# Down projections with the activations held still: 512 weight columns moving, sums kept with tokens on partitions and turned at the end of each MLP

## The reference, cut to what matters

```python
def squared_relu_mlp(hn, w_up, w_down):
    return jnp.square(jax.nn.relu(hn @ w_up)) @ w_down
...
        h = h + mix
        h = h + squared_relu_mlp(rms_norm(h, norm_mlp_g[i]), w_up[i], w_down[i])
        gate = jax.nn.sigmoid(rms_norm(h, norm_ple_g[i]) @ w_ple_gate[i])
        h = h + (p[i] @ w_ple_proj[i]) * gate
```

## Time and profile before

| what | value |
|---|---|
| runs, median of 3 | 2349.45 us (2348.93 to 2349.71) |
| profiled execution, first to last instruction (span) | 2346.1 us |
| profiled execution's own time | not listed apart from its span; the runs' median is 3.35 us above the span |
| TensorE busy | 2324.9 us, 99% |
| VectorE, ScalarE busy | 1534.6 us (65%), 1252.6 us (53%) |
| mean granted TensorE clock | 0.998 |

### The profile page before, as it was taken

One profiled execution on the slowest core, in us unless ns is written; L12 is line 12 of the kernel. 1 busy time (PEld: TensorE's weight loads), 2 busy tenths in 40 slices (PEclk: granted clock), 3 DMA queues, 4 the chain that ended last, 5 costly groups with the idle time before them and its releaser, 6 DMA issues.

```text
span 2346.1 us, 39851 instructions
## 1 busy us (share of the span) xinstructions
PE 2324.9 (99%) x13964; PEld 2078.5 (89%) x13964; DVE 1534.6 (65%) x1848; ACT 1252.6 (53%) x1616; POOL 77.1 (3%) x73
## 2 busy tenths in 40 slices
PE   8999999999999999999999999999999999999998
PEld 7999998888888888888888888888888888888887
DVE  8899776556556555668676666765555555556666
ACT  6876655445445435556666666555444444445454
POOL 0046100000000000000000000000000000000000
PEclk9999999999999999999999999999999999999999
DMA  8555465655655665665555555565556556556553
GB/s 254 181 181 161 154 206 172 195 179 190 194 189 182 191 199 179 188 205 174 186 179 157 176 170 177 180 190 179 189 196 188 180 194 198 179 184 202 186 166 122
DMA packets 432334, 431.24 MB, mean 184 GB/s; under 512 B 13312, under 2 KB 430208, under 8 KB 432256
## 3 DMA queue, kind: packets, MB, share of 16 engines
q1 hardware_dynamic: 431968, 429.97, 58.1%
q10 hardware_dynamic: 288, 0.23, 0.0%
HBM read 428.05 MB, written 2.10 MB: 183 GB/s over the span
## 4 chain that ended last, share of the span: by engine, by line
PE 97%; DVE 1%; ACT 1%; DMA 1%; issue 0%; DVEq 0%; ACTq 0%; SPq 0%
PE ps L492 54%; PE ps L498 28%; PE ps L533 3%; PE ps L534 3%; PE ps L535 3%; PE ps L490 2%; PE ps L497 1%; PE O L803 1%; DVE spl L1337 1%; DMA raw<-in_w_o 0%; PE O L654 0%; PE Z L628 0%; ACT spl L861 0%; PE Z L637 0%; PE ps L707 0%
## 5 line engine op out<-in xcount | busy, mean ns | idle before, releaser
L1337 DVE TENSOR_TENSOR spl<-raw,spl 128x1024 fp32r<-128x1024 f32 x797 | 938.6, 1222 | 579.5 <-ACT spl L861 572.2
L861 ACT ACTIVATE spl<-raw 128x1024 fp32r<-128x1024 f32 (+1 forms) x811 | 817.3, 1054 | 686.5 <-PE ps L498 593.7
L492 PE MATMUL ps<-XA,spl 128*128 128x512 f32 x2816 | 705.0, 392 | 7.3 <-DVE spl L1545 6.7
L492 PE MATMUL ps<-XB,spl 128*128 128x512 f32 x2784 | 711.5, 392 | 0.0
L492 PEld LDWEIGHTS ps<-XA,spl 128*128 128x128 f32 x2816 | 505.1, 189 | 91.5 <-issue 7.4
L492 PEld LDWEIGHTS ps<-XB,spl 128*128 128x128 f32 x2784 | 491.4, 188 | 75.6
L498 PEld LDWEIGHTS ps<-XB,spl 128*128 128x128 f32 x2784 | 394.5, 191 | 39.0
L498 PEld LDWEIGHTS ps<-XA,spl 128*128 128x128 f32 x2816 | 387.3, 191 | 31.4
L498 PE MATMUL ps<-XB,spl 128*128 128x256 f32 x2784 | 402.6, 281 | 0.0
L498 PE MATMUL ps<-XA,spl 128*128 128x256 f32 x2816 | 393.8, 282 | 0.0
L1373 DVE TENSOR_TENSOR tv<-cross,ps 128x512 f32<-128x512 f32 x181 | 123.2, 681 | 13.2 <-ACT cross L861 13.0
(11 more groups left out here) (207 smaller groups left out, 1531.6 us busy)
## 6 DMA issues: line engine op xcount, KB each, us to landing
raw<-in_w_up SPq DMA_DIRECT2D x256, 512.0 KB, 4.8
raw<-in_w_down SPq DMA_DIRECT2D x256, 512.0 KB, 5.2
raw<-in_w_qkv SPq DMA_DIRECT2D x96, 512.0 KB, 4.4
raw<-in_w_gate SPq DMA_DIRECT2D x64, 512.0 KB, 4.6
raw<-in_w_in SPq DMA_DIRECT2D x63, 512.0 KB, 4.7
raw<-in_w_out SPq DMA_DIRECT2D x32, 512.0 KB, 3.6
raw<-in_w_o SPq DMA_DIRECT2D x32, 512.0 KB, 4.8
raw<-in_w_proj SPq DMA_DIRECT2D x8, 512.0 KB, 4.1
```

What stands on the lines that cost most here:

```text
L492: pe.matmul(ps[:, b + o, :], w[:, q, 0, c], x[:, kt, :, :], start=start, stop=False)
L861: return act.activation(out, in_, ACT.Copy, scale=scale)
L1337: dve.tensor_tensor(s[:, :, 1, :], raw[:, m % NRAW, :, :], s[:, :, 0, :].bitcast(F32), ALU.subtract).then_inc(lo_ready, 1)
```

## The change

The 256 down-projection chunks become 2 x 128 rows of 512 output columns. The hidden activations are now stationary (128 tokens at a time), and 512 weight columns move: 12 matmuls a chunk, each with 512 moving columns. The result has tokens on the partitions, 512 channels wide. For each 512 channels and each quarter, DVE alone takes it out of PSUM into a buffer `acc` in SBUF (`collect`: a copy in the first quarter, an addition after that). In the last quarter TensorE turns `acc` in 128 x 128 blocks (`turn`: eight transposes for 512 channels, 32 a layer), DVE adds the turned block from PSUM to `h` (`take_turned`), and the residual chain follows. The turn of one block of 512 channels stands in the middle of the next block's matmuls; the last one stands between steps j = 1 and j = 2 of the gate's `first_pair`.

```diff
 def down(f):                                     # SP
     with sp.Fori(0, 4) as i:
-        for s in range(2):
-            load_group(m + 32 + 4 * s, f * 8 + i, w_down[layer], i * 512 + 256 * s, row0=f * D)
+        for c in range(8):
+            src = w_down[layer, bass.ds(f * D + 2 * c * P, 2 * P), bass.ds(i * 512, 512)]
+            load(m + 32 + c, f * 8 + i, src.rearrange("(t p) n -> p t n", p=P))
...
+def down(s, m, it, hid, tiles, mid=None):        # PE
+    b = 2 * s
+    for c in range(8):
+        if c == 4 and mid is not None:
+            mid()
+        if tiles is not None:
+            pe.wait_ge(*tiles[c])
+        lo_there(pe, m + c, it)
+        w = spl[:, (m + c) % NSPL, :, :, :]
+        for q in range(2):
+            for t in range(2):
+                x = [hid[:, 2 * c + q, k, t * P:(t + 1) * P] for k in range(2)]
+                for n, (xh, wh) in enumerate(((0, 0), (1, 0), (0, 1))):
+                    mm = pe.matmul(ps[:, b + t, :], x[xh], w[:, 2 * q:2 * q + 2, wh, :],
+                                   start=(c == 0 and q == 0 and n == 0), stop=(c == 7 and q == 1 and n == 2))
+        mm.then_inc(chunk_used, 1)
+
+def turn(g, hidx, i):                            # PE
+    pe.wait_ge(sum_ready, g + 56 + 2 * i + 2)
+    for k in range(2):
+        if hidx + 2 * i + k >= 2:
+            pe.wait_ge(res_ready, hidx + 2 * i + k - 1)
+        for j in range(2):
+            for t in range(2):
+                c = (4 * i + 2 * k + j) * P
+                mm = pe.transpose(O[:, k, j * T + t * P:j * T + (t + 1) * P], acc[:, t, c:c + P], ident[:, :])
+        mm.then_inc(turned, 1)
...
+    for i in range(4):                           # PE, last quarter
+        pe.wait_ge(sum_ready, g + 54 + 2 * i)
+        tiles = [(up_tiles, u + 24 + c + 1) for c in range(8)] if i == 0 else None
+        down(i % 2, m + 224 + 8 * i, 0, hid, tiles, None if i == 0 else lambda: turn(g, hidx, i - 1))
...
-    first_pair(g, m, x, after_res(f_in), lambda: stats(norm))
+    first_pair(g, m, x, after_res(f_in), lambda: stats(norm), mid=lambda: turn(*last, 3), sums=g - 2)
...
+    for i in range(4):                           # ACT, last quarter
+        for q in range(8):
+            split(m + 224 + 8 * i + q + NSPL)
+            if i > 0 and 4 <= q < 6:
+                k = 2 * i + q - 6
+                residual((res_ready, hidx + k + 1), hidx + k, 2 * k, n, X)
...
+def collect(s, m, it, col, before, fresh):       # DVE
+    dve.wait_ge(chunk_used, it * 8 + (m + 8))
+    if not fresh:
+        dve.wait_ge(sum_ready, before)
+    for t in range(2):
+        a = acc[:, t, bass.ds(col, 512)]
+        if fresh:
+            r = dve.tensor_copy(a, ps[:, 2 * s + t, :])
+        else:
+            r = dve.tensor_tensor(a, a, ps[:, 2 * s + t, :], ALU.add)
+        r.then_inc(sum_ready, 1)
...
+def take_turned(hidx, k, f, n, X):               # DVE
+    dve.wait_ge(turned, hidx // 24 * 8 + k + 1)
+    ht = h[:, 2 * k:2 * k + 2, :]
+    dve.tensor_tensor(ht, ht, O[:, k % 2, :].rearrange("p (o n) -> p o n", o=2), ALU.add).then_inc(res_ready, 1)
+    dve.wait_ge(res_ready, hidx + k + 1)
+    residual(f + k, 2 * k, n, X)
...
+    for i in range(4):                           # DVE, last quarter
+        for q in range(8):
+            if q == 7:
+                collect(i % 2, m + 224 + 8 * i, 0, 512 * i, g + 40 + 2 * i + 2, False)
+            split(m + 224 + 8 * i + q + NSPL)
+            if i > 0 and 4 <= q < 6:
+                take_turned(hidx, 2 * i + q - 6, f_out, n, X)
...
-gates(G_GATE0, C_GATE0, 0, 24, H_GATE0, 2, 3, XB)                # DVE; ACT alike
+gates(G_GATE0, C_GATE0, 0, 24, H_GATE0, 2, 3, XB, {
+    4: lambda: take_turned(H_MLP0, 6, 16, 2, XA), 5: lambda: take_turned(H_MLP0, 7, 16, 2, XA)})
```

More of the change, by code:

```diff
@@ L67 @@
 CHUNKS = 812
[L69 removed]
+H_MLP0, H_GATE0, H_OUT1, H_MLP1, H_GATE1 = 0, 8, 16, 24, 32
 NDG = 22
@@ L290, in crossed @@
         def crossed(g):
-            return g - (32 if g >= G_MLP0 else 0) - (8 if g >= G_OUT1 else 0)
+            return g - sum(n for first, n in ((G_MLP0, 32), (G_GATE0, 32), (G_OUT1, 8), (G_GATE1, 32)) if g >= first)
         def lo_there(engine, m, it):
@@ new lines, in mlp, with ups, downs @@
+            def mlp(g, m, x, hid, f_in, norm, u, hidx):
+                def ups(f):
+                    whole(g, f * 16, m, f * 8, x, sums=f * 16 + (g - 2))
+                    whole(g + 1, f * 16, m + 4, f * 8, x)
+                    with pe.Fori(1, 4) as i:
+                        for s in range(2):
+                            whole(g + s, f * 16 + i * 2, m + 4 * s, f * 8 + i, x)
+                def downs(f):
+                    with pe.Fori(0, 2) as j:
+                        for s in range(2):
+                            pe.wait_ge(sum_ready, f * 16 + j * (3 + s) + (g + 7 + s))
+                            tiles = [(up_tiles, f * 8 + (u + c + 1)) for c in range(8)] if s == 0 else None
+                            down(s, m + 32 + 8 * s, f * 8 + j * 2, hid, tiles)
@@ L943, in up, with gate @@
                 copy(hid[:, bass.ds(t0, 2), 0, :], tv[:, :, :]).then_inc(up_hi, 1)
-            def gate(g, gi, m, it, k, hidx, t0, n, X, norm_n=None, first=False):
-                group(g, gi, m, it, first, 2)
+            def gate(g, gi, m, it, k, hidx, t0, n, X, norm_n=None, first=False, steps={}):
+                group(g, gi, m, it, first, 2, steps)
                 if norm_n is not None:
@@ L975, in mlp @@
                 with act.Fori(0, 4) as i:
-                    for s in range(2):
-                        group(g + 8 + s, i * 2, m + 32 + 4 * s, i)
+                    period(m + 32, i, 8)
                 with act.Fori(1, 3) as f:
@@ L1349, in period, with group @@
                     split(m + NSPL + q, it)
-            def group(g, gi, m, it, first=False, later=0, steps={}):
+            def group(g, gi, m, it, first=False, later=0, steps={}, ci=None):
                 if not first:
@@ L1432, in up, with proj @@
                 dve.wait_ge(up_tiles, u + 1)
-            def down(g, gi, m, it, hidx, t0, first=False, later=0, steps={}):
+            def proj(g, gi, m, it, hidx, t0, first=False, later=0, steps={}):
                 group(g, gi, m, it, first, later, steps)
@@ L1459, in out_groups @@
                     for s in range(2):
-                        down(g + s, 0, m + 4 * s, 0, hidx + s, 2 * s, True, steps=first)
+                        proj(g + s, 0, m + 4 * s, 0, hidx + s, 2 * s, True, steps=first)
                         residual(f + s, 2 * s, n, X)
@@ L1469, in mlp @@
                 for s in range(2):
[L1470 removed]
+                    up(g + s, 0, 0, m + 4 * s, 0, u + s, 2 * s, hid, norm_in if s == 0 else None, True)
                 with dve.Fori(1, 4) as i:
                     for s in range(2):
[L1473 to L1476 removed]
+                        up(g + s, i * 2, i * 2, m + 4 * s, i, i * 2 + (u + s), i * 4 + 2 * s, hid)
+                downs(g, m, 0, True)
                 with dve.Fori(1, 3) as f:
```

123 lines of the change are left out of this document (55 added, 68 removed).

## The result

The changed kernel takes **2355.57 us** (median of 9 runs, 2353.74 to 2357.02), the kernel before 2349.45 us in the runs beside it (9 runs): a ratio of 1.0025, 95% interval 1.0016 to 1.0035. The forecast was 2357.6 us with a range of 2350 to 2368, so the sign and the size came out. How they came about did not follow the forecast in every step, and errors of opposite sign partly cancelled each other.

What follows compares the result with a forecast made beforehand. The prediction took TensorE's matmul stream as the bound. Matmuls -12.4, transposes +5.3 and waits at the gate +15.2 gave +8.1 us, a span of 2354.2 us and, with 3.35 us above the span, 2357.6 us (range 2350 to 2368).

Steps and rivals of the forecast that it cites:

- Part 1: Down matmuls on TensorE: 12 of 227.5 ns a chunk replace 16, saving 48.5 ns in each of 256 chunks, -12.4 us.
- the prediction's own sign of being wrong: Down matmul spacing other than 227.5 ns, no wait at the gate, or waits in the quarters before would show it wrong.
- Part 2: Transposes on TensorE: one pass each at 0.11 us, 48 in the open over two layers, +5.3 us.
- Part 3: Sums on ACT and DVE: both lose work, hidden in idle time; no collection waited for in the first three quarters.
- Part 4: Last down quarter and gate's start: queued DVE and ACT work makes TensorE wait 7.6 us per layer, +15.2 us.
- Wait A: Gate's second chunk waits 2.4 us a layer for the PSUM pair that DVE is still collecting.
- wait B: Gate's step j = 3 gets its input 5.2 us later; TensorE spends 0.9 on turn(3) and waits 4.3.
- the step on the clock: At the gate, TensorE's granted clock was to be still 1.00 behind the second wait, of about 4.3 us.
- this fall as a rival: TensorE's clock falls at the gate in both layers, costing up to 2 x 2.5 us: 2362.6 us; chance 0.10.
- Two passes: Each transpose on TensorE takes two passes, 0.22 us, 10.6 us in all: 2362.8 us; chance 0.20.
- Waits covered: Gate waits cost nothing and all 64 transposes count: -5.4 us, 2344.1 us; chance 0.17, in whole or part.
- A gap in the moving operand: Down matmuls moving two runs of 256 columns pay for the gap: up to +37 us, 2394 us; chance 0.03.

Runs made afterwards that it cites:

- The first two experiments: Changed kernel with turn(0) to turn(2) ahead of the third down chunk, not the fifth: 2352.29 us; changed kernel with only turn(3) one gate step earlier: 2344.18 us.
- the first experiment: Changed kernel with turn(0) to turn(2) ahead of the third down chunk instead of the fifth, residual chains moved likewise, turn(3) unmoved: 2352.29 us, ratio 1.0011.

## Why the prediction was right, point by point

- **Part 1 was mis-sized, the mechanism held.** Four matmuls less a chunk is a gain that nothing covers, and weights move no slower than activations. No gap cost showed up in the moving operand. The gain is 15.0 us instead of 12.4. For the chunk after I took 227.5 ns for each matmul from blocks of 32, whose start behind 256 columns is slow, and a stream of 384 runs at 226.75. A difference of 0.3% in a term that stands 3072 times in the kernel is 2.3 us, nearly what the whole change weighs in a layer (2.86). By the letter, the prediction's own sign of being wrong, a spacing other than 227.5, came true. The terms as written also give 47.6 ns a chunk, not 48.5; that takes the 2778.6 ns of 689.10 us for 248 chunks, and the down chunks alone took 2779.4.
- **Part 2 held.** One pass, and the price was right: 0.11 us, taken from line 628 rather than from line 727, although 727 has the type and the shape; 0.113 with the matmul behind, 0.109 for one more. 48 open transposes are 5.4 us, forecast 5.3. The page of the Trainium skill weighed there ("TensorE: Matmul & The Clock Gate", section Terms) has a transpose mode four times as fast for FP32, and does not say than what. The trace does not bear out the estimate made of it, a quarter of 0.22 us or 0.055: a transpose costs half of the 0.22.
- **Part 3 held.** DVE and ACT lose work, there is no wait in the first three quarters, and loads in wider rows (packets down from 432,334 to 366,810 on the two pages) bring TensorE no wait for a chunk in the stretch.
- **Part 4 held in mechanism, and both waits were forecast too long.** Wait A costs 1.48 us a layer instead of 2.4 (1.33 of wait and 0.15 of starting again), wait B 4.5 instead of 5.2 (with the eight transposes that it covers), because the queue of DVE repeats every 4.30 us and not 4.73. The first two experiments show each wait alone, by taking it away.
- **What failed is the step on the clock**, "granted clock still 1.00 behind the second". I had this fall as a rival at 0.10 and up to 2.5 us a layer. It came, in both layers, at 1.67 us (2.5 in one layer of the first experiment, so the price I gave was the upper end). The row for it was on the table: 0.70 some 4 us after dense work ended, and a wait B of 4.3 us. No row spoke against it. It should have been in the sum.
- **The other rivals.** Two passes: refuted. Waits covered: not in this kernel, but reached by moving the turns. A gap in the moving operand: refuted by 226.75 ns, where moving activations without a gap settle at 226.8.

Put together by what was measured: -15.0 + 48 x 0.113 + 2 x (1.48 + 4.5 + 1.67) = +5.7 us, which is what the two stretches show. The forecast was +8.1: matmuls and the two waits were too dear by 2.6, 1.8 and 1.4, the transposes too cheap by 0.1, and the clock was missing with 3.3. So the total was nearer than its terms: the missing clock hid more than half of what the others had too much, and that is luck.

## What to carry to other kernels

A cheaper matmul stream can lose all its gain at the one place where its results have to get back into the layout of the next stage: here -15.0 us became +6.1, and moving the same instructions two chunks and one step ahead made it -7.5. So when results leave TensorE by a longer way, count the queue of the engines that carry them (period by period, from start to start), and place the work so that the last consumer still has that long. Where an idle wait of TensorE like wait B (3.5 us here) can't be avoided, add the lower clock behind it to its price (1.7 to 2.5 us here), or try needless matmuls that fill it. And take a price from a whole stretch with and without the thing: the window of 0.79 us around eight transposes missed an eighth of their cost.

## What the runs showed of the hardware

- A plain float32 transpose of 128 x 128 is one instruction, while a plain float32 product of the same shape is two. In a stream it costs 0.109 us, 0.113 with the matmul behind that is followed late. Its own record says 273 ns. The Trainium skill ("TensorE: Matmul & The Clock Gate", Part 4 on the transpose) gives about 275 ns for one in bf16 in a kernel; the trace agrees for float32.
- In the changed kernel the clock falls not in the wait but after it: TensorE works for 1 us at 1.00 and then at a mean of 0.53 for 3.6 us. What that costs is not fixed. With wait A gone (the first experiment) the clock fell within the same wait B in the first layer, a mean of 0.79 in the row below, and the whole chunk with its statistics ran at the lower level (1055.26 to 1060.82, 5.56 us instead of 3.03, so 2.5 lost); in the second layer it took as long as in the changed kernel (2261.95 to 2266.65, 4.70). The nine runs of the changed kernel have a mean granted clock of 0.995 to 0.997: the two at 0.995 took 2356.4 us, the five at 0.997 took 2354.5 in the mean. Wait A, 1.33 us, was followed by no fall.

```profile
1051.80:1055.20 3.40, 0.00 (x0) 0.00 (x0) 2.56 (x7) 2.37 (x4) 0.00 (x0) 0.79 0.46 155
```

- 512 moving columns settle at 226.7 ns from matmul to matmul, whether weights move or activations. Behind 32 matmuls with 256 columns the first few are slower, some 25 ns together, so that blocks of 32 come to 227.5. The cause is open.
